# A two-block model on one core: the first block's GpSimd arithmetic moved to VectorE and TensorE

## The chip, the core and the metric

The kernel runs on 1 core of a Trainium2 chip. The metric is the device time of one execution in microseconds (us); the kernel before takes 1670.41 us, the median of three runs (1668.84 to 1670.69). The engines are named as in the profile: PE is TensorE, DVE is VectorE, ACT is ScalarE, POOL is GpSimd, SP is SyncE, which issues most of the loads.

## What is computed

256 tokens of width 1024 pass through two blocks. The first block, the one that matters here, is:

```
mod = silu(c) @ w_ada + b_ada                      # 6 x 1024: sh1, sc1, gt1, sh2, sc2, gt2
h = rms_norm(x, g_norm_mix) * (1 + sc1) + sh1
proj = h @ w_in                                    # q, k, v of 8 forgetting and of 8 stick-breaking heads, 8 gates
log_fcum = cumsum(log_sigmoid(f_logit + b_forget))
forgetting head:      p = softmax(q k / 8 + log_fcum[q] - log_fcum[k], causal);  o = p v
stick-breaking head:  z = q k / 8;  mask k < q
                      rest = reverse cumsum of log_sigmoid(-z) masked to 0, less itself
                      a = exp(log_sigmoid(z) + rest) masked to 0;  o = a v
x = x + gt1 * (norm(o) @ w_out)
h2 = rms_norm(x, g_norm_ffn) * (1 + sc2) + sh2
x = x + gt2 * peer(h2)     # per token and head: scores of 2 x 128 keys, top 16 of 16 x 16,
                           # the 16 chosen rows of expert_down and expert_up (16384 x 1024 each)
```

The second block (a differential and block-sparse attention layer, a gated linear attention layer and two feed-forward layers) follows and is not touched.

## The kernel before

All queues are written out by hand. Each engine has a list of steps (`Queue`), executed strictly in the order in which Python appends them; a step waits on semaphores for its inputs, and everything behind it on that engine waits too. Nothing is scheduled by a planner, so the order of the code is the order on the engines.

**Weights** come as tiles of 1024 x 512 (2 MB) into four buffers W0 to W3. `load_on` issues the loads on SP strictly in the order of the list of tiles, each when the tile that held its buffer is done (`wdone`). The tiles of the first block in order: w_ada 0, 2, 1, 3, w_in 0, 1, 2, w_ada 4, w_in 3, w_ada 5, 6, w_in 4, w_ada 7, w_in 5, w_ada 8, 9, w_out 0, w_query 0, w_out 1, w_query 1, 2, 3, w_ada 10, 11. Products use fp32r operands in two parts: ACT copies a quarter of a tile to WH, and DVE or POOL forms WL = W - WH (`split_piece`, four pieces a tile); a product is then three matmuls for each of 8 row blocks.

**Work beside the products** stands in the deque `behind`: pieces of splits (`later_split`) and, for w_ada tiles 4 to 9, pieces of `ada_rows` (`later_ada`, `later_close`). `tick(n)` puts the next n of them on the engines after a group of matmuls, `take` the rest that a product needs, and `drain` all. `ada_rows` makes one 512-wide piece of the modulation as a row: DVE accumulates the w_ada rows of 4 blocks times silu(c) in LNV, ACT scales the other 4 blocks, POOL adds them up (`sums`), and a product with a matrix of ones (`close`) sums over the partitions; only then is the tile's buffer free.

**Order around the change.** After w_in 0 and 1 (queries and keys of the stick-breaking heads) come w_in 2 (their values), 3 and 4 (forgetting queries and keys); between their groups of 24 matmuls stand the steps of the 8 stick-breaking heads: `sb_first` (scores, ACT abs, exp and ln, two DVE operations, two POOL multiplications by the mask), `sb_second` (the reverse cumulative sum as products, one DVE addition, ACT exp, two POOL multiplications), `sb_third` (the product with the values). Then comes w_in 5 (forgetting values) with the first four of the ten steps of `attention` (scores, reductions, exponents, three transposes of the head before, product with the values) between its halves, and a loop over the rest with `tick(2)` after each. nG holds minus the cumulative log gates for the queries; a DVE operation adds it and the mask to the scores. After the loop come the norms of the heads, the product with w_out, the second norm, and the PEER layer: the query of tokens 0 to 127 with w_query 0, `choose(0, 0, 1)` (the top 16 of the first head, all on DVE), the other query tiles (`first_query`, `query_groups`), then 256 gathers on POOL (1 MB each, 8 buffers of EB) with a DVE dot product (line 78), ACT steps and two products for each. The first gather waits for `tk1`, the end of the second `first_query`; gathers 2 and 3 for w_query 0, 4 and 5 for w_query 2, 6 and 7 for the end of w_query 3, later ones for the product that frees their buffer.

Of the kernel before, what the change touches and what calls it, by code (L numbers as in the profile page):

```python
# [182 lines left out]
def build(nc, A, out, C1, C2):  # L183
    ctx = ExitStack()
    with ctx:
# [32 lines left out]
        with ExitStack() as under:  # L218
            W.append(under.enter_context(nc.sbuf_tensor("W3", [128, 8, 512], F32)))
            WH = [under.enter_context(nc.sbuf_tensor(f"WH{i}", [128, 8, 512], F32R)) for i in range(3)]  # L220
            AH = under.enter_context(nc.sbuf_tensor("AH", [128, 2, 8, 256], F32R))
            AL = under.enter_context(nc.sbuf_tensor("AL", [128, 2, 8, 256], F32R))
        EB = sb("EB", [128, 16384])
# [488 lines left out]
        def ada_rows(j, direct=()):  # L712
# [7 lines left out]
            def some(ks, kp):  # L720
                def step():
# [7 lines left out]
                    for k in kp:  # L729
                        t["a"] = act(lambda e: e.activation(tile.w[:, k, :], tile.w[:, k, :], ACT.Copy, scale=silu_c[:, k:k + 1]),  # L730
                                     t_cb, tile.arrived, ordered=False)
                return step

            def sums():
                w = tile.w
                pool(lambda e: e.tensor_tensor(w[:, 4, :], w[:, 4, :], w[:, 5, :], ALU.add), t["a"])
                if not direct:
                    pool(lambda e: e.tensor_tensor(w[:, 6, :], w[:, 6, :], w[:, 7, :], ALU.add))
                    pool(lambda e: e.tensor_tensor(w[:, 4, :], w[:, 4, :], w[:, 6, :], ALU.add))
                t["p"] = pool(lambda e: e.tensor_tensor(w[:, 4, :], w[:, 4, :], acc, ALU.add), t["d"])  # L740
                acc_free[half] = (t["p"],)
# [13 lines left out]
            a, b = some((0, 1), (4, 5)), some((2, 3), () if direct else (6, 7))  # L755
            return [(cond, a), (cond, lambda: (b(), sums()))], (cond, close)
# [7 lines left out]
        def forget_gates():  # L764
# [21 lines left out]
            yield  # L786
            b = bank()
            mm(PS[b][:, 0:8], [(tri, nl[:, 0, :])], t_nl, *bank_free[b])
            tk = mm(PS[b][:, 8:16], [(ones, nl[:, 0, :]), (tri, nl[:, 1, :])])
            t = dve(lambda e: e.tensor_scalar(nG, PS[b][:, 0:16].rearrange("p (t h) -> p t h", t=2), -1.0, None, ALU.mult), tk)  # L790
            bank_free[b] = (t,)
            t_gates["nG"] = t
            yield
# [43 lines left out]

        gate = forget_gates()
# [11 lines left out]
        def attention(heads, q_of, k_of, v_of, vw, out_bank, scale, LB, PT, maps=1, gates=False, lam=None, tokens=(), base=0, done=None,  # L850
                      taken=None, values_in=lambda: ()):

            NL, NP = len(LB), len(PT)
            MX, SM = (a[:, base:] for a in (MXA, SMA))
            lb_free = [taken() if taken else () for _ in range(NL)]
            pt_free = [taken() if taken else () for _ in range(NP)]
            n = heads
            state = {}
            done["next"] = 0

            def scores(h):
                for m in range(maps):
                    i = h * maps + m
                    b = bank()
                    pe.wait(*tokens, *bank_free[b])
                    for t in range(2):
                        nk = 128 * (t + 1)
                        o = PS[b][:, 128 * t:128 * t + nk]
                        q, k = q_of(i)[:, 128 * t:128 * (t + 1)], k_of(i)[:, 0:nk]
                        if gates:  # L870
                            pe.plain(lambda e, o=o, q=q, k=k: e.matmul(o, q, k, start=True, stop=False))
                            g0 = nl[:, 0, i:i + 1].broadcast_to([128, 128])
                            g1 = nl[:, 1, i:i + 1].broadcast_to([128, 128])
                            if t == 0:
                                tk = pe(lambda e, o=o, g0=g0: e.matmul(o, g0, tri, start=False, stop=True), ordered=False)
                            else:
                                pe.plain(lambda e, o=o, g0=g0: e.matmul(o, g0, tri_ones, start=False, stop=False))
                                tk = pe(lambda e, o=o, g1=g1: e.matmul(o[:, 128:256], g1, tri, start=False, stop=True), ordered=False)
                        else:
                            tk = mm(o, [(q, k)])  # L880
                    L = LB[i % NL]
                    free = lb_free[i % NL]
                    if gates:
                        for t in range(2):
                            c = slice(0, 128) if t == 0 else slice(128, 384)
# [3 lines left out]
                    else:  # L889
                        td = dve(lambda e, b=b, L=L: e.scalar_tensor_tensor(  # L890
                            out=L, in0=PS[b][:, 0:384], scalar=scale, in1=maskF, op0=ALU.mult, op1=ALU.add), tk, *free)
                    bank_free[b] = (td,)
                    for t in range(2):
                        c = slice(0, 128) if t == 0 else slice(128, 384)
                        j = 2 * i + t
                        tm = dve(lambda e, c=c, L=L, j=j: e.tensor_reduce(MX[:, j:j + 1], L[:, c], X_AXIS, ALU.max, negate=True))
                    for t in range(2):
                        c = slice(0, 128) if t == 0 else slice(128, 384)
                        j = 2 * i + t
                        ta = act(lambda e, c=c, L=L, j=j: e.activation(L[:, c], L[:, c], ACT.Exp, bias=MX[:, j:j + 1],  # L900
                                                                       accum_out=SM[:, j:j + 1]), tm, ordered=False)
                    state[i] = ta

            def weights(h):

                tk = [state[h * maps + m] for m in range(maps)]
                j = 2 * h * maps
                tr_ = dve(lambda e: e.reciprocal(SM[:, j:j + 2 * maps], SM[:, j:j + 2 * maps]), *tk)
                if maps == 1:
                    return tk[0]  # L910
# [1314 lines left out]
```

How the kernel before makes its waits and increments, by code:

```python
    def wait(self, *tokens):  # L100
        for sem, value in tokens:
            if value > self.seen.get(sem.name, 0):
                self.seen[sem.name] = value
                self.steps.append(lambda e, s=sem, v=value: e.wait_ge(s, v))
# [1 line left out]
    def __call__(self, make, *tokens, ordered=True):  # L106
        self.wait(*tokens)
        if ordered:
            self.wait(self.last)
        self.n += 1
        self.steps.append(lambda e, m=make(LATER), s=self.sem: m(e).then_inc(s, 1))
        return self.last
# [4 lines left out]
    def dma(self, make, slot, *tokens):  # L118
        self.wait(*tokens)
        slot.n += 16
        self.steps.append(lambda e, m=make(LATER), s=slot.sem: m(e).then_inc(s, 16))
        return (slot.sem, slot.n)
```

## Time and profile before

| | us |
|---|---|
| median of three runs | 1670.41 |
| lowest and highest | 1668.84, 1670.69 |
| the profiled execution | 1669.52 |
| its span on the core | 1667.7 |
| PE busy, share of the span | 1367.8 (82%) |
| DVE busy | 1112.0 (67%) |
| ACT busy | 545.0 (33%) |
| POOL busy | 461.7 (28%) |

The span falls into three stretches: up to about 316 us the first block as far as the last query tile, from there to about 975 us the stream of gathers, and then the second block. Engine shares are averages over these and say little by themselves; each stretch has to be read by what its engines wait for.

### The profile page before, as it was taken

The numbers are of one execution on the slowest core, as the hardware profiler recorded it, in microseconds if no ns is written. First come the engines' busy times: TensorE is split into PE (matmuls) and PEld (weight loads), VectorE is DVE, ScalarE is ACT, GpSimd is POOL, SyncE is SP. The second block draws the span as 40 slices with busy tenths as digits, with TensorE's granted clock in tenths as the row PEclk, the third lists the DMA queues.
The fourth block names the chain that finished last, engine by engine and source line by source line (L and its number), as shares of the span: only waits on it lengthen the run. The fifth ranks groups of instructions, "written<-read, shape, count | busy, mean of one in ns | idle before, by whom it ended". The sixth has DMA issues, their size and how long they took to land.

```text
span 1667.7 us, 17183 instructions
## 1 busy us (share of the span) xinstructions
PE 1367.8 (82%) x6192; PEld 956.3 (57%) x6192; DVE 1112.0 (67%) x2013; ACT 545.0 (33%) x1046; POOL 461.7 (28%) x397
## 2 busy tenths in 40 slices
PE   5887779778777777777777778968999989889997
PEld 5876668523223222322222237856999878679996
DVE  6665756588888678877555555556765577768554
ACT  1454423322221123122111133542544253435431
POOL 1153405245444344444344401100111023001110
PEclk8898889999999899999999988989999999999999
DMA  9554524799999999999999934324555442345450
GB/s 365 194 201 152 202 76 168 288 421 409 421 421 414 417 422 388 384 421 421 421 421 421 422 160 152 102 76 147 184 202 181 174 154 104 124 177 192 173 191 26
DMA packets 116628, 433.16 MB, mean 260 GB/s; under 512 B 6832, under 2 KB 7088, under 8 KB 83520
## 3 DMA queue, kind: packets, MB, share of 16 engines
q0 software_dynamic: 36864, 268.45, 39.0%
q1 hardware_dynamic: 79392, 162.51, 27.4%
q8 instruction: 49, 0.80, 0.2%
q10 hardware_dynamic: 288, 1.11, 0.2%
q14 instruction: 35, 0.29, 0.0%
HBM read 431.00 MB, written 1.05 MB: 259 GB/s over the span
## 4 chain that ended last, share of the span: by engine, by line
PE 48%; DMA 23%; DVE 19%; ACT 6%; issue 2%; POOL 1%; SPq 0%; DVEq 0%; ACTq 0%; POOLq 0%
PE PS L45 47%; DMA EB<-in_experts,EI 22%; DVE EB L78 5%; DVE WL L75 4%; ACT BIG L24 2%; ACT WH L24 1%; PE PS L84 1%; DMA W<-in_w_ada 1%; DVE Y L75 1%; DVE GV L75 1%; DVE XL L75 1%; ACT EB L24 1%; DVE X L63 1%; DVE LNV L63 1%; ACT XH L24 1%
## 5 line engine op out<-in xcount | busy, mean ns | idle before, releaser
L45 PE MATMUL PS<-EB,BIG 128*128 128x512 f32 x1024 | 496.9, 630 | 168.0 <-ACT BIG L24 168.0
L45 PEld LDWEIGHTS PS<-EB,BIG 128*128 128x128 f32 x1024 | 190.8, 197 | 469.4 <-ACT BIG L24 285.0
L78 DVE CUSTOM_DVE_ANT_0 EB<-EB,Y 128x1024 f32<-128x1024 f32 x256 | 313.5, 1224 | 145.8 <-DMA EB<-in_experts,EI 144.6
L39 POOL DMA_INDIRECT EB<-in_experts,EI x256 | 291.2, 1137 | 394.2 <-PE PS L45 378.5
L75 DVE TENSOR_TENSOR WL<-W,WH 128x1024 fp32r<-128x1024 f32 x228 | 297.2, 1352 | 111.4 <-ACT WH L24 111.0
L24 ACT ACTIVATE WH<-W 128x1024 fp32r<-128x1024 f32 x240 | 237.2, 1048 | 81.6 <-PE PS L45 75.8
L45 PE MATMUL PS<-XH,WH 128*128 128x256 f32 x832 | 243.0, 292 | 10.6 <-DVE WL L75 10.0
L45 PE MATMUL PS<-XH,WL 128*128 128x256 f32 x832 | 236.9, 285 | 0.0
L45 PE MATMUL PS<-XL,WH 128*128 128x256 f32 x832 | 236.7, 285 | 0.0
L24 ACT ACTIVATE BIG<-BIG 128x2 f32<-128x2 f32 (+1 forms) x136 | 31.1, 228 | 442.2 <-DVE BIG L78 441.8
L45 PEld LDWEIGHTS PS<-XH,WH 128*128 128x128 f32 x832 | 161.1, 194 | 14.0 <-DVE WL L75 11.1
L45 PEld LDWEIGHTS PS<-XL,WH 128*128 128x128 f32 x832 | 161.2, 194 | 1.9 <-issue 1.4
L45 PEld LDWEIGHTS PS<-XH,WL 128*128 128x128 f32 x832 | 161.2, 194 | 0.0
L45 PE MATMUL PS<-WH,XH 128*128 128x512 f32 x288 | 124.0, 431 | 22.2 <-DVE XL L75 15.2
L75 POOL TENSOR_TENSOR AL<-Y,AH 128x512 fp32r<-128x512 f32 x28 | 36.3, 1296 | 331.2 <-DVE AH L66 331.2
L24 ACT ACTIVATE BIG<-K,BIG 128x128 f32<-128x128 f32 x256 | 100.3, 393 | 59.1 <-DVE BIG L75 57.8
L45 PE MATMUL PS<-WL,XH 128*128 128x512 f32 x288 | 118.4, 411 | 0.0
L45 PE MATMUL PS<-WH,XL 128*128 128x512 f32 x288 | 118.1, 410 | 0.0
L45 PE MATMUL PS<-WL,AH 128*128 128x512 f32 x256 | 101.4, 396 | 0.0
L45 PE MATMUL PS<-WH,AH 128*128 128x512 f32 x256 | 100.8, 394 | 0.0
L45 PE MATMUL PS<-WH,AL 128*128 128x512 f32 x256 | 100.1, 391 | 0.0
L45 PEld LDWEIGHTS PS<-WH,XH 128*128 128x128 f32 x288 | 57.5, 200 | 38.3 <-DVE XL L75 17.7
(176 smaller groups left out, 1496.7 us busy)
## 6 DMA issues: line engine op xcount, KB each, us to landing
W<-in_ffn_w SPq DMA_DIRECT2D x32, 2048.0 KB, 8.5
W<-in_w_ada SPq DMA_DIRECT2D x12, 2048.0 KB, 12.3
W<-in_w_in SPq DMA_DIRECT2D x6, 2048.0 KB, 13.6
W<-in_hy_w_in SPq DMA_DIRECT2D x6, 2048.0 KB, 13.7
W<-in_gla_w_in SPq DMA_DIRECT2D x6, 2048.0 KB, 7.9
W<-in_w_query SPq DMA_DIRECT2D x4, 2048.0 KB, 10.4
W<-in_w_out SPq DMA_DIRECT2D x2, 2048.0 KB, 8.0
EB<-in_experts,EI POOLq DMA_INDIRECT x256, 11.2
```

The costliest lines, as they stand in the source:

```text
L24: return lambda e: e.activation(*a, **k)
L39: return lambda e: e.indirect_dma_start(*a, **k)
L45: return lambda e: e.matmul(*a, **k)
L63: return lambda e: e.scalar_tensor_tensor(*a, **k)
L75: return lambda e: e.tensor_tensor(*a, **k)
L78: return lambda e: e.tensor_tensor_reduce(*a, **k)
L84: return lambda e: e.transpose(*a, **k)
```

## The change

- `ada_rows`: DVE accumulates 6 blocks instead of 4 (three pieces of two blocks in `behind`, before two pieces), the last two blocks are products of silu(c), broadcast, with the tile (fp32, 512 columns each), and `close` adds the product of ones with LNV. ACT's scaling and POOL's sums are gone.
- Stick-breaking heads: the four POOL multiplications are gone; a product of the identity with a strict mask (0 or -1e30), both fp32r in the new tile MR, is added to the scores of each of the two diagonal tiles.
- Forgetting heads: the function `attention` becomes `forgetting`. The causal mask is a product of the identity with 384 columns, the row maxima are read from PSUM, and ACT takes the exponent from PSUM. The two DVE operations that added nG and the mask are gone, and so is the calculation of nG.
- The WL parts of w_out 1, w_query 1 and w_query 2 are made by DVE instead of POOL.
- `choose(0, 0, 1)` stands ahead of `drain()` instead of behind it.

```diff
@@ ada_rows
-            def some(ks, kp):
+            def some(ks):
...
-                    for k in kp:
-                        t["a"] = act(lambda e: e.activation(tile.w[:, k, :], tile.w[:, k, :], ACT.Copy, scale=silu_c[:, k:k + 1]),
-                                     t_cb, tile.arrived, ordered=False)
...
-            def sums():
-                w = tile.w
-                pool(lambda e: e.tensor_tensor(w[:, 4, :], w[:, 4, :], w[:, 5, :], ALU.add), t["a"])
...
-                t["p"] = pool(lambda e: e.tensor_tensor(w[:, 4, :], w[:, 4, :], acc, ALU.add), t["d"])
...
             def close():
                 b = bank()
-                tk = mm(PS[b][:, :], [(silu_c[:, k:k + 1].broadcast_to([128, 128]), tile.w[:, k, :]) for k in direct] +
-                        [(ones, tile.w[:, 4, :])], t["p"], *bank_free[b])
+                tk = mm(PS[b][:, :], [(silu_c[:, k:k + 1].broadcast_to([128, 128]), tile.w[:, k, :]) for k in (6, 7)] + [(ones, acc)],
+                        t["d"], tile.arrived, *bank_free[b])
...
-            a, b = some((0, 1), (4, 5)), some((2, 3), () if direct else (6, 7))
-            return [(cond, a), (cond, lambda: (b(), sums()))], (cond, close)
+            return [(cond, some((0, 1))), (cond, some((2, 3))), (cond, some((4, 5)))], (cond, close)
@@ forgetting, scores
-                            td = dve(lambda e, c=c, t=t, b=b, L=L, i=i: e.scalar_tensor_tensor(
-                                out=L[:, c], in0=PS[b][:, c], scalar=nG[:, t, i:i + 1], in1=maskF[:, c],
-                                op0=ALU.add, op1=ALU.add), tk, *free)
...
+                pe.plain(lambda e: e.matmul(PS[b][:, 0:384], ident_a, causal_a, start=True, stop=False))
...
+                    tm = dve(lambda e: e.tensor_reduce(MXA[:, 2 * h + t:2 * h + t + 1], PS[b][:, cols[t]], X_AXIS, ALU.max, negate=True),
+                             tk, ordered=False)
@@ sb_first
-            pool(lambda e: e.tensor_tensor(zb[:, 0:128], zb[:, 0:128], maskS, ALU.mult), dd)
-            zst[h] = (pool(lambda e: e.tensor_tensor(zb[:, 256:384], zb[:, 256:384], maskS, ALU.mult)), dd)
+            pe.plain(lambda e: e.matmul(PS[b][:, 0:128], ident_a, strict_a, start=False, stop=True))
...
+            zst[h] = (dd,)
@@
-        later_split(wout[1], pool)
+        later_split(wout[1])
...
-        later_split(wq[1], pool)
-        later_split(wq[2], pool)
+        later_split(wq[1])
+        later_split(wq[2])
         next(query)
         tick(1)
         norm_x1.last()
         t_xt = norm_x1.tokens
         next(query)
-        drain()
         for step in choose(0, 0, 1):
             step()
+        drain()
```

What it moves on DVE is told here at three places. The names are those of the buffers: W, WH and WL with the buffer's number, LNV the accumulator of `ada_rows`, PS the PSUM banks, ST the row maxima, EB the exponents.

DVE between the first two forgetting heads, before: w_in 5 has just begun, and w_ada 8 (in W0) and w_ada 9 (in W3) are accumulated behind the maxima of head 0.

```order
L75 TENSOR_TENSOR GV<-GV,PS0 128x512
L63 SCALAR_TENSOR_TENSOR EB<-PS2,ST,K1 128x128
L63 SCALAR_TENSOR_TENSOR EB<-PS2,ST,K1 128x256
L69 TENSOR_REDUCE ST<-EB 128x1 x2
L66 COPY BIG<-PS1 128x512
L72 TENSOR_SCALAR LNV<-W0,ST 128x512
L63 SCALAR_TENSOR_TENSOR LNV<-W0,ST,LNV 128x512 x3
L72 TENSOR_SCALAR LNV<-W3,ST 128x512
L63 SCALAR_TENSOR_TENSOR LNV<-W3,ST,LNV 128x512 x3
```

The same place in the changed kernel, up to the maxima of head 1 and 2.

```order
L69 TENSOR_REDUCE ST<-PS0 128x1 x2
L66 COPY BIG<-PS3 128x512
L75 TENSOR_TENSOR GV<-GV,PS1 128x512
L72 TENSOR_SCALAR LNV<-W0,ST 128x512
L63 SCALAR_TENSOR_TENSOR LNV<-W0,ST,LNV 128x512 x5
L72 TENSOR_SCALAR LNV<-W3,ST 128x512
L63 SCALAR_TENSOR_TENSOR LNV<-W3,ST,LNV 128x512
L69 TENSOR_REDUCE ST<-PS2 128x1 x2
L60 RECIPROCAL ST<-ST 128x2
L66 COPY EB<-PS3 128x384
L69 TENSOR_REDUCE ST<-PS1 128x1 x2
```

The addition of the closed w_ada 7 row (GV) used to stand ahead of head 0's maxima and now stands behind them, and the maxima of head 1 stand behind the first two of the six operations on w_ada 9.

DVE in the loop over the forgetting heads, in the changed kernel: the splits of w_out 0 (WL0) and w_out 1 (WL3) between the maxima of heads 5, 6 and 7.

```order
L75 TENSOR_TENSOR WL0<-W0,WH0 128x1024 x2
L69 TENSOR_REDUCE ST<-PS1 128x1 x2
L60 RECIPROCAL ST<-ST 128x2
L66 COPY EB<-PS2 128x384
L75 TENSOR_TENSOR WL0<-W0,WH0 128x1024
L75 TENSOR_TENSOR WL3<-W3,WH1 128x1024
L69 TENSOR_REDUCE ST<-PS3 128x1 x2
L60 RECIPROCAL ST<-ST 128x2
L69 TENSOR_REDUCE ST<-PS6 128x8
L75 TENSOR_TENSOR WL3<-W3,WH1 128x1024 x2
```

Before, all four WL0 pieces stood together ahead of head 3, and there was no WL3 piece on DVE at all. Now one WL0 piece stands ahead of head 3's maxima and seven pieces follow in the loop.

DVE around `choose(0, 0, 1)`, the difference: from MAX to the CAST into EI it is the choice of the first head, WL1 is of w_query 1 and WL0 of w_query 2.

```order
 L63 SCALAR_TENSOR_TENSOR Y<-Y,ST,GV 128x512 x2
+L75 TENSOR_TENSOR WL<-W,WH 128x1024
 L75 TENSOR_TENSOR XL<-PS,XH 128x4x128 x2
 L48 MAX LNV<-BIG 128x8
```

```order
 L63 SCALAR_TENSOR_TENSOR LNV<-LNV 128x16
 L66 CAST EI<-LNV 128x16
+L75 TENSOR_TENSOR WL<-W,WH 128x1024 x7
 L78 ISA EB,BIG<-EB,Y 128x1024
```

One WL piece now stands ahead of the last XL parts, and the other seven stand behind the whole choice; before, POOL made all eight.

## Rows read from the trace of the kernel before

**Rows 1.** Windows: us, busy time (instructions) of each engine, granted clock, DMA share, GB/s.

```profile
300.00:316.00 16.00, 15.02 (x94) 12.88 (x94) 12.53 (x36) 2.57 (x6) 0.00 (x0) 0.91 0.37 142
400.00:500.00 100.00, 74.76 (x161) 28.78 (x162) 83.65 (x211) 24.05 (x69) 47.33 (x41) 1.00 1.01 421
```

**Rows 2.** Timeline of POOL: start, us, operation, idle time before and its releaser.

```profile
257.81 19.18 POOL L75 TENSOR_TENSOR WL<-W,WH 128x1024 fp32r<-128x1024 f32 x8 [50.33 <-ACT WH L24]
281.31 1.11 POOL L39 DMA_INDIRECT EB<-in_experts,EI  x1 [4.33 <-PE PS L45]
316.61 0.94 POOL L39 DMA_INDIRECT EB<-in_experts,EI  x1 [22.00 <-PE PS L45]
```

**Rows 3.** Timeline of PE, rows that begin after a wait or mark a stage.

```profile
71.73 0.83 PE L45 MATMUL PS<-ST,K 128*128 128x8 f32 x6 [1.68 <-DVE ST L75]
126.67 0.58 PE L45 MATMUL PS<-XH,WH 128*128 128x256 f32 x1 [3.44 <-DVE WL L75]
170.31 1.22 PE L45 MATMUL PS<-W,K 128*128 128x512 f32 x1 [8.84 <-POOL W L75]
191.81 0.90 PE L84 MATMUL PS<-K,EB 128*128 128x128 f32 x3 [5.33 <-ACT EB L24]
209.77 0.63 PE L84 MATMUL PS<-K,Y 128*128 128x128 f32 x2
259.59 0.50 PE L45 MATMUL PS<-WH,XH 128*128 128x512 f32 x1 [1.60 <-DVE XL L75]
268.23 0.60 PE L84 MATMUL PS<-K,EB 128*128 128x128 f32 x4
307.00 1.98 PE L45 MATMUL PS<-EB,BIG 128*128 128x512 f32 x4 [0.98 <-ACT BIG L24]
```

**Rows 4.** Groups by form, 60 to 280 us: busy, mean ns, idle before.

```profile
L24 ACT ACTIVATE WH<-W 128x1024 fp32r<-128x1024 f32 x36 | 35.8, 1050 | 1.6 <-DMA W<-in_w_in 1.4 <-issue 0.2
L75 DVE TENSOR_TENSOR WL<-W,WH 128x1024 fp32r<-128x1024 f32 x24 | 29.5, 1266 | 15.3 <-ACT WH L24 15.3
L45 PE MATMUL PS<-BIG 128*128 128x128 f32 x32 | 7.2, 311 | 0.0
```

**Rows 5.** Timeline of DVE in the heads and splits of the first block.

```profile
94.00 2.55 DVE L63 SCALAR_TENSOR_TENSOR LNV<-W,ST,LNV 128x512 f32<-128x512 f32 x3
184.37 4.62 DVE L75 TENSOR_TENSOR WL<-W,WH 128x1024 fp32r<-128x1024 f32 x4
189.09 0.87 DVE L63 SCALAR_TENSOR_TENSOR EB<-PS,ST,K 128x128 f32<-128x128 f32 x2
190.00 0.74 DVE L69 TENSOR_REDUCE ST<-EB 128x1 f32<-128x128 f32 x2
```

**Rows 6.** Timeline of DVE in the choice of experts: beside POOL's splits, and later without.

```profile
265.09 2.56 DVE L75 TENSOR_TENSOR GV<-LNV 128x256 f32<-128x256 f32 x1
270.20 4.45 DVE L72 TENSOR_SCALAR LNV<-LNV 128x16 uint32<-128x16 uint32 x2
280.22 0.17 DVE L66 CAST EI<-LNV 128x16 int32<-128x16 f32 x1
311.84 0.42 DVE L75 TENSOR_TENSOR GV<-LNV 128x256 f32<-128x256 f32 x1
330.05 0.39 DVE L72 TENSOR_SCALAR LNV<-LNV 128x16 uint32<-128x16 uint32 x2
```

**Rows 7.** DMA issues by SP in a short window: KB each, us to landing.

```profile
W<-in_w_out SPq DMA_DIRECT2D x1, 2048.0 KB, 7.9
```

**Rows 8.** Windows, columns as in rows 1: four stretches of the first block.

```profile
75.33:153.69 78.36, 65.54 (x374) 58.12 (x373) 44.88 (x57) 37.57 (x61) 34.01 (x45) 0.87 0.45 161
153.69:209.77 56.08, 39.53 (x212) 33.62 (x210) 39.11 (x71) 25.29 (x59) 21.43 (x12) 0.86 0.52 188
191.80:198.00 6.20, 6.19 (x29) 5.90 (x30) 2.27 (x7) 3.88 (x8) 1.72 (x1) 0.57 0.70 254
268.23:292.16 23.93, 23.24 (x198) 22.83 (x196) 13.05 (x22) 4.19 (x7) 12.68 (x8) 1.00 0.74 284
```

More of the change, by code:

```diff
@@ L222, in build @@
             AL = under.enter_context(nc.sbuf_tensor("AL", [128, 2, 8, 256], F32R))
+        with ExitStack() as under:
+            under.enter_context(nc.sbuf_tensor("EB_a", [128, 15744], F32))
+            MR = under.enter_context(nc.sbuf_tensor("MR", [128, 640], F32R))
         EB = sb("EB", [128, 16384])
@@ L848, in build, with forgetting @@
         t_sb_in = (act.last, dve.last, pool.last)
[L850 to L857, printed above, removed]
+        def forgetting(LB, PT, values_in, *tokens):
+            lb_free = [(fox_done["sb"],) for _ in LB]
+            pt_free = [(fox_done["sb"],) for _ in PT]
@@ L858, in attention @@
             state = {}
-            done["next"] = 0
+            cols = [slice(0, 128), slice(128, 384)]
             def scores(h):
[L862 to L885, printed above, removed]
-                            td = dve(lambda e, c=c, t=t, b=b, L=L, i=i: e.scalar_tensor_tensor(
-                                out=L[:, c], in0=PS[b][:, c], scalar=nG[:, t, i:i + 1], in1=maskF[:, c],
-                                op0=ALU.add, op1=ALU.add), tk, *free)
[L889 to L910, printed above, removed]
[L911 to L918 removed]
+                b = bank()
@@ new lines, in scores @@
+                pe.wait(*tokens, t_ident, *bank_free[b])
+                pe.plain(lambda e: e.matmul(PS[b][:, 0:384], ident_a, causal_a, start=True, stop=False))
+                g0, g1 = (nl[:, t, h:h + 1].broadcast_to([128, 128]) for t in range(2))
+                k = KF[:, h // 2, :]
+                pe.plain(lambda e: e.matmul(PS[b][:, 0:128], QF[:, h, 0:128], k[:, 0:128], start=False, stop=False))
+                pe.plain(lambda e: e.matmul(PS[b][:, 0:128], g0, tri, start=False, stop=False))
@@ L920, in turned @@
+                L = LB[h % len(LB)]
+                for t in range(2):
+                    j = 2 * h + t
+                    ta = act(lambda e: e.activation(L[:, cols[t]], PS[b][:, cols[t]], ACT.Exp, bias=MXA[:, j:j + 1], accum_out=SMA[:, j:j + 1]),
+                             tm, *lb_free[h % len(LB)], ordered=False)
+                bank_free[b] = (ta,)
+                state[h] = ta
             def turned(h):
-                tk = weights(h)
-                L = LB[(h * maps) % NL]
+                dve(lambda e: e.reciprocal(SMA[:, 2 * h:2 * h + 2], SMA[:, 2 * h:2 * h + 2]), state[h])
@@ L946, in attention @@
+                v = lambda t: V[:, t, h * 64:(h + 1) * 64]
+                mm(PS[4][:, h * 64:(h + 1) * 64], [(P[:, 0:128], v(0))], state["pt", h], *values_in(), *bank_free[4], *bank_free[5])
+                tk = mm(PS[5][:, h * 64:(h + 1) * 64], [(P[:, 128:256], v(0)), (P[:, 256:384], v(1))])
+                pt_free[h % len(PT)] = (tk,)
+                return tk
+            after_values = 0
+            for i in range(10):
+                if i < 8:
                     scores(i)
-                if 0 <= i - 1 < n:
+                if 0 <= i - 1 < 8:
@@ L1027, in build @@
         fm_tile(win[4], evac_copy(lambda c: KF[:, c:c + 2, :]), hook=step_sb)
-        fox = attention(8, lambda i: QF[:, i, :], lambda i: KF[:, i // 2, :],
-                        lambda h, t: V[:, t, h * 64:(h + 1) * 64], 64, 4, 1.0,
-                        [buf(i) for i in (6, 7, 8, 9)], [buf(i) for i in (0, 1, 2, 3, 4)],
-                        gates=True, tokens=(act.last, dve.last, t_gates["nG"]), done=fox_done, taken=lambda: (fox_done["sb"],),
-                        values_in=lambda: t_vf)
+        fox = forgetting([buf(i) for i in (5, 6, 7, 8)], [buf(i) for i in (0, 1, 2, 3, 4)], lambda: t_vf, act.last, dve.last, t_gates["nl"])
         later_ada(8)
```

70 lines of the change are left out of this document (27 added, 43 removed).

## The prediction, made before the changed kernel ran

> **What bounds the kernel now.** I read the windows first, then the timelines of POOL, PE and DVE up to 330 us. In the middle stretch the DMA engines are full: 421 GB/s at a share of 1.01 from 400 to 500 us, with DVE busy for 84 of 100 us [rows 1]. The stream begins for good at 316.61 us, when POOL has waited 22 us for PE [rows 2]: it waits for the end of w_query 3, which frees the last two gather buffers. Just before it, from 300 to 316 us, the DMA share is 0.37 [rows 1]. So the first block is worth to the total exactly what it does to the end of w_query 3, and nothing behind that point changes: same gathers, same order, same second block. DVE's or POOL's busy time in the first block is worth nothing by itself. Up to that point the path is PE's queue with its waits: 3.44 us for a WL part at 126.67, 8.84 us for POOL's sums at 170.31, 5.33 us for ACT's exponents at 191.81 [rows 3]. From 75.33 to 153.69 PE is busy for 65.54 of 78.36 us at a mean clock of 0.87, that is for about 20 us at the lower of its two levels, 1.2 instead of 2.4 GHz [rows 8].
>
> **Part 1, to the end of w_ada 7's product.** Before, this is at 153.69 us, where the window of 78.36 us ends. Of the 78.36 us in front of it 12.8 are waits; the low clock takes half of some 20 us, 10.2; PE's work at full clock is 65.5 - 10.2 = 55.3 us [rows 8]. Nearly all of the waits come from POOL or ACT's scaling, and they go. The products for nG (0.83 us, 0.7 without the pipeline) with the wait of 1.68 us ahead of them go too [rows 3]: 2.4 us, so that the stretch begins at 72.9 (estimate from the start of the products at 75.33). Added on PE: an fp32 product of 512 columns is two records, and four take 1.98 us [rows 3], so some 0.86 to 0.99 us each; two more for each of four tiles are 6.9 us. The 16 mask products of 128 columns are in no row. An fp32 product of this width is two records, and the records run one behind another at some 0.11 us, well under the mean of 0.311 us that contains the pipeline [rows 4]; I bound one mask product by 0.06 and 0.21 us and take 0.13, 2.1 us in all (1.0 to 3.4). The order also puts 24 matmuls of w_in 5 (5.6), the scores of the first forgetting head (1.7) and one sb_third (0.6) ahead of this product, which stood behind it: 7.9 us. New waits: w_in 4's first group needs WL parts that stand on DVE behind the close of w_ada 5 and behind a head's DVE and ACT work, as at 126.67 before [rows 3]; walking DVE's and ACT's queues there gives 6.1 us more than the group takes, with 0.8 us each for a bank and for the clock behind it: 7.9 us with rounding. The sum: 72.9 + 55.3 + 6.9 + 2.1 + 7.9 + 7.9 = 153.0 us. **Gain 0.7 us** (2.6 more if the clock stays up).
>
> DVE's 12 added accumulations are 0.85 us each, three in 2.55 us [rows 5]; in this part DVE is busy for 44.9 of 78.4 us [rows 8] and has the room.
>
> **Part 2, from there to the first transposes of the heads' norm (209.77).** Before: 56.08 us [rows 8], of which 8.84 is the wait for POOL's sums [rows 3]. That wait goes, but two loads take its place. w_ada 9 is loaded into the buffer that this product frees, and a lone 2 MB load lands after 7.9 us [rows 7]. Before, DVE had the maxima of head 1 behind all of w_ada 9, too, but PE was held by POOL anyway. Now: 8.0 (landing), 1.6 (two DVE operations), 0.8 (maxima of head 1, 0.74 in [rows 5]), 1.0 (exponents on ACT), 0.3 (hand-overs), then on PE 0.5 (transposes), 2.8 (12 matmuls), 2.6 (closing w_ada 8): 17.6 us. Only then can w_out 0 be loaded: 8.0, then WH 1.05 on ACT, WL 1.2 on DVE [rows 4], and behind it in DVE's queue the maxima of head 3, 0.75, and ACT's exponents, 1.0: 12.0 us to the transposes of head 3, the place of 191.81 before. From there the loop took 18.0 us, to 209.77 [rows 3]. In it stand now seven WL pieces of 1.16 us (four in 4.62) and five times 0.87 us for nG and mask less [rows 5], 8.1 - 4.4 = 3.7 us more of DVE work. Because each pair of pieces waits for its WH copies and holds the next head's maxima, I walked the queues step by step: exponents of head 5 end at 8.0, of head 6 at 14.4, of head 7 at 20.0, the last WL piece at 23.3, the row of norms at 24.8 us. 17.6 + 12.0 + 24.8 = 54.4 us. **Gain 1.7 us**; if the clock falls behind the first of these waits, as it did behind 191.81 (0.57 for 6.2 us [rows 8]), a loss of 1.1.
>
> **Part 3, norms to w_query 0.** The same steps on the same engines, but one WL piece now ahead of the XL parts on which the product at 259.59 waits; ACT's copy for it is ready, so it moves them by what it takes less a gap of 0.5 us: **loss 0.7 us**.
>
> **Part 4, the query tiles.** This is the largest term. Before, the 24 matmuls of w_query 0 and the first 24 of w_query 1 end at 268.23, 8.64 us after 259.59 [rows 3], while POOL makes the WL parts in 2.40 us each [rows 2]. Now three of the four WL pieces of w_query 1 stand on DVE behind `choose(0, 0, 1)`. That took 20.7 us, from 259.6 to the cast at 280.22 [rows 6]. Three groups of its rows were long beside POOL: the addition 2.56 instead of 0.42, the two shifts 4.45 instead of 0.39 us [rows 6], and the casts around them likewise; with the later durations of the same rows it takes 10.8 us. Then WL: 12.0, 13.1, 14.3 us, and 0.7 us for the last matmuls: 15.0 us instead of 8.6, **loss 6.4 us**. PE has no slack to return it: from 268.23 to 292.16 us it is busy for 23.2 of 23.9 us [rows 8], and w_query 3's end follows from there. The clock may fall behind this wait of 5.6 us, which costs 2.4 us more; I take half, 1.2. The choice is ready ten microseconds earlier, but the first gather waits for the second query's scores, which stand on PE behind this wait. It was issued at 281.31 before [rows 2], 21.7 us after 259.59; now, by PE, at some 21.9 us: it hardly moves.
>
> **Sum:** -0.7 - 1.7 + 0.7 + 6.4 + 1.2 = +5.9 us, on the profiled execution's 1669.5: 1675.4. The median of the runs is 0.9 us above it: **1676.3 us**.
>
> **A rule that speaks for the change.** DVE's rows beside POOL were slow: 4.45 against 0.39 us [rows 6]. The Trainium skill, GPSIMD Engine Reference, Specifications, says that GpSimd shares its SBUF interfaces with VectorE and contends with instructions that have two SBUF inputs or run in a two-port mode. On this the trace agrees. The rule with the choice taken as the path would give these ten microseconds as a gain, some 1660 us; by the rows they only shorten the wait of part 4, and its chance is within that of rival A.
>
> **The rivals.** *A: DVE has room and PE keeps its lead.* DVE is busy for 39.1 of 56.1 us in part 2 [rows 8], and its rows get shorter without POOL. If the splits fit into the loop's gaps, it stays at 18.0 us, 6.8 less than I walked, and with the clock up in part 1 2.6 more goes, and the 1.2: 1676.3 - 10.6 = 1665.7, faster. It decides at whether the loop ends within 20 us of head 3's transposes. Against it: the WL pieces stand in queue ahead of maxima, and ACT's copies ahead of exponents. *B: the wait in part 4 is made up* before w_query 3: PE waits 3 us for WL of w_query 3 and about 1 us for ACT behind it, and parts 1 and 2 are at their better ends. About -5 us: 1671, no change. Against it: these waits hang on the scores of w_query 2, which are late as well. *C: the clock falls behind each new wait* (parts 2 and 4) and mask products cost 0.21 us: +2.8, +1.2, +1.3, 1681.6.
>
> **Chances.** The forecast with its near surroundings (1673.8 to 1679) 0.47, C 0.19, B 0.21, A 0.13. A measurement of this kernel can tell some 0.2%, 3.3 us, from no change. Faster by more: 0.13; within: 0.22; slower by more: 0.65. The range is from inside A, 1666, to beyond C, 1683.
>
> **What would show it.** In the changed profile: no ACT or POOL wait on PE up to 150 us, w_ada 7 closed near 153; a wait of some 4 us for ACT before head 1's transposes and of 5 to 6 before head 3's; the norm's first transposes near 208; PE waiting 5 to 6 us for WL in the first group of w_query 1, right behind the products of w_query 0, while DVE runs the choice in about 11 us; the stream of gathers restarting near 322 and as long as before. It would be wrong if that first group ran without a wait, or if the loop of the forgetting heads took less than 20 us.

## The result, and the profile after

The changed kernel takes 1675.7 us (median of 12 runs, 1672.1 to 1678.6), the kernel before 1668.6 us (12 runs, 1666.0 to 1671.6) beside it. The ratio is 1.0040, 95% interval 1.0028 to 1.0051: **slower by 4.7 to 8.5 us**. The forecast was +5.9 us and 1676.3 us. Most times below come from one profiled execution of each kernel. The profiled execution of the changed kernel took 1672.6 us.

The stages of the prediction, as windows of the changed kernel: to the close of w_ada 7, from there to the norm's first transposes, the loop over the forgetting heads inside that, the first product with w_query 0, the way from its second product to the end of w_query 1's first group, the last 18 of the 24 matmuls of that group, and the way on to the stream. The columns are those of [rows 1].

```profile
72.60:152.14 79.54, 73.79 (x446) 62.73 (x445) 48.55 (x68) 31.43 (x53) 0.00 (x0) 0.98 0.45 159
152.14:207.29 55.15, 38.24 (x187) 31.93 (x185) 31.88 (x59) 18.47 (x46) 0.00 (x0) 0.81 0.53 191
182.66:207.29 24.63, 18.18 (x97) 16.84 (x97) 15.38 (x29) 13.69 (x31) 0.00 (x0) 0.71 0.49 180
246.97:254.38 7.41, 7.41 (x24) 5.56 (x24) 5.06 (x11) 1.13 (x4) 0.00 (x0) 0.77 0.01 2
259.81:275.76 15.95, 10.44 (x49) 9.16 (x50) 14.94 (x43) 6.17 (x7) 0.00 (x0) 0.79 0.39 131
271.87:275.76 3.89, 3.89 (x19) 3.89 (x20) 3.89 (x4) 0.00 (x0) 0.00 (x0) 0.52 0.25 91
275.76:323.87 48.11, 42.26 (x318) 39.05 (x316) 20.32 (x46) 13.09 (x22) 5.80 (x7) 0.96 0.58 219
```

POOL does nothing in these windows up to the gathers. The timeline of PE shows the waits that have come in place of those for POOL in [rows 3], with the rows that mark the stages.

```profile
72.60 0.40 PE L45 MATMUL PS<-WH,XH 128*128 128x512 f32 x1
...
118.09 0.39 PE L45 MATMUL PS<-XH,WH 128*128 128x256 f32 x1 [3.98 <-DVE WL L75]
...
149.41 1.88 PE L45 MATMUL PS<-W,ST 128*128 128x512 f32 x4
151.12 1.02 PE L45 MATMUL PS<-LNV,K 128*128 128x512 f32 x2
...
163.45 0.90 PE L84 MATMUL PS<-K,EB 128*128 128x128 f32 x3 [4.80 <-ACT EB L24]
...
182.66 0.90 PE L84 MATMUL PS<-K,EB 128*128 128x128 f32 x3 [5.66 <-ACT EB L24]
...
207.29 1.12 PE L84 MATMUL PS<-K,Y 128*128 128x128 f32 x4 [0.89 <-DVE Y L75]
...
259.81 0.50 PE L45 MATMUL PS<-WH,XH 128*128 128x512 f32 x1 [2.24 <-DVE XL L75]
...
271.87 0.58 PE L45 MATMUL PS<-XH,WH 128*128 128x256 f32 x1 [5.51 <-DVE WL L75]
```

PE's two waits for ACT's exponents, at 163.45 and 182.66 us, go back to two loads. DVE waits 3.25 us for the landing of w_ada 9, of which two operations stand ahead of the maxima of head 1. ACT waits 10.08 us for the landing of w_out 0, whose first split piece stands ahead of the maxima of head 3.

```profile
160.65 0.49 DVE L72 TENSOR_SCALAR LNV<-W,ST 128x512 f32<-128x512 f32 x1 [3.25 <-DMA W<-in_w_ada]
161.17 0.75 DVE L63 SCALAR_TENSOR_TENSOR LNV<-W,ST,LNV 128x512 f32<-128x512 f32 x1
161.84 0.61 DVE L69 TENSOR_REDUCE ST<-PS 128x1 f32<-128x128 f32 x2
```

```profile
178.82 1.06 ACT L24 ACTIVATE WH<-W 128x1024 fp32r<-128x1024 f32 x1 [10.08 <-DMA W<-in_w_out]
```

DVE at the choice of the first head: one WL piece, the XL parts, the choice with the two shifts in it, and then the WL pieces for which PE waits.

```profile
257.33 1.23 DVE L75 TENSOR_TENSOR WL<-W,WH 128x1024 fp32r<-128x1024 f32 x1 [4.08 <-ACT WH L24]
258.47 1.28 DVE L75 TENSOR_TENSOR XL<-PS,XH 128x512 fp32r<-128x512 f32 x2
259.86 0.30 DVE L48 MAX8 LNV<-BIG 128x8 f32<-128x128 f32 x1
...
266.73 0.39 DVE L72 TENSOR_SCALAR LNV<-LNV 128x16 uint32<-128x16 uint32 x2
...
270.52 0.17 DVE L66 CAST EI<-LNV 128x16 int32<-128x16 f32 x1
270.60 8.03 DVE L75 TENSOR_TENSOR WL<-W,WH 128x1024 fp32r<-128x1024 f32 x7
```

And POOL, the first gather and the one that begins the stream:

```profile
280.35 1.11 POOL L39 DMA_INDIRECT EB<-in_experts,EI  x1 [217.29 <-PE PS L45]
...
323.87 0.94 POOL L39 DMA_INDIRECT EB<-in_experts,EI  x1 [21.73 <-PE PS L45]
```

The choice takes 10.83 us instead of 20.75 [rows 6], and the first gather leaves 1 us earlier. The stream begins 7.26 us later than at 316.61 [rows 2], and the last gather leaves at 969.45 instead of 961.41. The two profiled spans differ by 3.1 us only: in the one of before the last eight products on the gathered rows ran at the lower clock, for 6.38 instead of 3.70 us, and the four before them took 3.09 instead of 1.98 us, 3.8 us together. The medians differ by 7.2 us.

### The profile page after: what moved, and what is told of

Same layout as the page of the kernel before. It is cut to its first block, busy times and chain, and to the rows that moved or that the text cites. A ratio compares the mean times of both kernels' runs of the same rounds, so it can differ in the third digit from the quotient of the medians.

```text
span 1670.8 us, 17135 instructions
## 1 busy us (share of the span) xinstructions
PE 1381.0 (83%) x6234; PEld 967.0 (58%) x6234; DVE 1106.2 (66%) x2021; ACT 530.4 (32%) x1024; POOL 378.5 (23%) x329
## 4 chain that ended last, share of the span: by engine, by line
PE 48%; DMA 24%; DVE 19%; ACT 5%; issue 2%; SPq 0%; POOL 0%; DVEq 0%; ACTq 0%; POOLq 0%
PE PS L45 47%; DMA EB<-in_experts,EI 22%; DVE EB L78 5%; DVE WL L75 4%; ACT BIG L24 2%; DMA W<-in_w_ada 1%; ACT WH L24 1%; PE PS L84 1%; DVE Y L75 1%; DVE GV L75 1%; DVE LNV L63 1%; DVE XL L75 1%; ACT EB L24 1%; DVE X L63 1%; DVE ST L69 1%
## 5 line engine op out<-in xcount | busy, mean ns | idle before, releaser
L75 DVE TENSOR_TENSOR WL<-W,WH 128x1024 fp32r<-128x1024 f32 x240 | 310.3, 1341 | 119.4 <-ACT WH L24 119.0
L45 PEld LDWEIGHTS PS<-WH,XH 128*128 128x128 f32 x288 | 57.8, 201 | 39.2 <-DVE XL L75 18.4
## 6 DMA issues: line engine op xcount, KB each, us to landing
W<-in_w_ada SPq DMA_DIRECT2D x12, 2048.0 KB, 12.8
EB<-in_experts,EI POOLq DMA_INDIRECT x256, 11.3
```

The source lines that it names most:

```text
L45: return lambda e: e.matmul(*a, **k)
L75: return lambda e: e.tensor_tensor(*a, **k)
```

## The experiments

Two theories stood against each other. The first is the forecast's: what is late is PE's way to the end of w_query 3, through DVE's queue order, so the parts can be undone there. The second: the parts that moved to PE and DVE cost by themselves. Here is where each kernel stood in its profiled execution. "Head 3" is the start of its transposes, "norm" that of the norm's first transposes, the loop is the difference, "stream" is the gather after the long wait for PE; ratios are to the kernel before, with 95% intervals. The places are of one execution each; the column "stream" holds 1.6 us that go with the clock in the first product with w_query 0 and not with the edits (last section): that product was at full clock in the kernel before, in the early close with the splits on POOL, in the rows in two pieces and in both kernels with the rows as before.

| kernel | head 3 | norm | loop | stream | ratio |
|---|---|---|---|---|---|
| before | 191.81 | 209.77 | 18.0 | 316.61 | 1 |
| changed | 182.66 | 207.29 | 24.6 | 323.87 | 1.0040 (1.0028 to 1.0051) |
| WL of w_query 1 first | 183.35 | 207.98 | 24.6 | 317.37 | 1.0004 (0.9995 to 1.0013) |
| all WL pieces first | 183.60 | 207.84 | 24.2 | 318.82 | 0.9999 (0.9988 to 1.0010) |
| w_out 1 on POOL | 184.42 | 207.16 | 22.7 | 324.87 | 1.0047 (1.0035 to 1.0059) |
| all old splits on POOL | 183.04 | 205.77 | 22.7 | 313.94 | 0.9993 (0.9983 to 1.0002) |
| w_ada 8 closed early | 183.82 | 207.23 | 23.4 | 323.08 | 1.0030 (1.0018 to 1.0041) |
| closed early, splits on POOL | 181.74 | 203.24 | 21.5 | 310.15 | 0.9960 (0.9947 to 0.9973) |
| rows in two pieces | 184.44 | 203.36 | 18.9 | 318.17 | 0.9996 (0.9979 to 1.0014) |
| rows as before | 179.53 | 197.96 | 18.4 | 313.61 | 0.9960 (0.9947 to 0.9973) |
| rows as before, WL of w_query 1 first | 178.97 | 197.82 | 18.8 | 305.13 | 0.9925 (0.9904 to 0.9946) |
| masks alone | 179.99 | 197.18 | 17.2 | 306.23 | 0.9911 (0.9891 to 0.9930) |
| rows alone | 188.49 | 213.71 | 25.2 | 322.53 | 1.0023 (1.0009 to 1.0037) |

**The order at the choice.** Two kernels differ from the changed one only here.

```diff
+        take(wq[1])
         for step in choose(0, 0, 1):
             step()
         drain()
```

> The changed kernel with one edit: the four WL pieces of w_query 1 are made ahead of the choice of the first head, those of w_query 2 stay behind it. My theory: PE's wait of 5.51 us in the first group of w_query 1 is DVE's queue order and nothing else. It then goes whole, the 24 matmuls of w_query 0 and the first 24 of w_query 1 take 8.6 to 9.5 us instead of 15.95, the long gather stream restarts at 316.5 to 318 us instead of 323.87, and the time falls by 6 to 7 us, to that of the kernel before (ratio to it 0.999 to 1.001). Rival 1, a landing or ACT's WH copies hold the group: a wait of over 3 us stays, the ratio stays at 1.004. Rival 2, the wait is only moved to a later product (the choice is now later by 3.5 us): the group is short, the restart stays near 323.

The second has `drain()` ahead of the loop, as before.

> The changed kernel with the old order of the two lines: all seven WL pieces (w_query 1 and 2) ahead of the choice, which ends some 8 to 10 us later than 270.69. My theory, that only PE's path to the end of w_query 3 counts: the same as with w_query 1 alone ahead, restart 316.5 to 318 us, ratio 0.999 to 1.001; the first gather may come some us later than 280.35 and this costs nothing. Rival, that the early indices were worth something: the time is 2 to 4 us above that of the kernel with only w_query 1 ahead, because the first gathers are late.

Both as expected in the times; the two groups take 8.50 us, just under the 8.6 forecast, and the second kernel's stream begins at 318.82 us, 0.8 us behind the latest forecast. The window of the two products, with w_query 1's WL pieces first, is 8.50 us at full clock, where the changed kernel has 15.95:

```profile
260.57:269.07 8.50, 8.50 (x49) 7.42 (x49) 8.02 (x24) 6.17 (x7) 0.00 (x0) 1.00 0.15 34
```

The time falls by 0.36 to 0.41% of 1668.6, 6.0 to 6.8 us: part 4 of the prediction is settled. With all pieces first the first gather leaves at 279.66 instead of 275.79 us, and the two times are the same within their intervals: no gain of early indices can be seen here.

**The splits of w_out 1.**

```diff
-        later_split(wout[1])
+        later_split(wout[1], pool)
```

> The changed kernel with the WL parts of w_out 1 on POOL, as before; everything else stays on DVE. My theory: DVE's pieces ahead of the heads' maxima make the loop over the forgetting heads long (24.6 us from head 3's transposes to the norm's first transposes, 18.0 before). Three or four of eight pieces leave DVE: the loop takes 19 to 21 us, and the time falls by 3.5 to 5.5 us (ratio 1.001 to 1.002). Rival, ACT's WH copies ahead of the exponents set the loop, whoever subtracts: it stays at 23.5 to 24.6 us and the time does not move (1.004).

Missed. POOL has the four pieces, and the loop is shorter by 1.9 us, not by 3.6 to 5.6; of the time nothing came back.

```profile
196.07 2.45 POOL L75 TENSOR_TENSOR WL<-W,WH 128x1024 fp32r<-128x1024 f32 x1 [132.01 <-ACT WH L24]
199.18 6.96 POOL L75 TENSOR_TENSOR WL<-W,WH 128x1024 fp32r<-128x1024 f32 x3 [0.67 <-ACT WH L24]
```

DVE's part in w_out 1 is thus a small term; neither theory named the large one. This execution was 1.0 us late at the group of 118.09 already, 1.8 us at head 3, and the stream began 1.0 us later than in the changed kernel; by the two intervals a gain of more than 2 us is as good as excluded.

**All old splits on POOL again.**

```diff
-        later_split(wout[1])
+        later_split(wout[1], pool)
...
-        later_split(wq[1])
-        later_split(wq[2])
+        later_split(wq[1], pool)
+        later_split(wq[2], pool)
```

> The changed kernel with all WL parts that POOL made before (w_out 1, w_query 1 and 2) on POOL again; the modulation rows and both masks stay as changed. My theory: the loop shortens as with w_out 1 alone, the wait of 5.5 us in the first group of w_query 1 goes, and DVE's choice is slow again beside POOL (20 us instead of 10.8) without cost, since the first gather waits for PE. Restart at 312 to 314 us, the time 3 to 6 us below the kernel before (ratio 0.9965 to 0.998). Rival, the rows on PE and the masks cost by themselves: the ratio is 1.000 or above.

The wait in part 4 is gone, and the choice is slow again:

```profile
267.79 4.47 DVE L72 TENSOR_SCALAR LNV<-LNV 128x16 uint32<-128x16 uint32 x2
...
277.81 0.17 DVE L66 CAST EI<-LNV 128x16 int32<-128x16 f32 x1
```

4.47 us for the pair of shifts against 0.39 without POOL: the choice takes 20.7 us beside POOL in this kernel and 10.8 in the changed one. The addition in it with both inputs in the SBUF took 2.57 us at 262.67 against 0.42. That agrees with the Trainium skill, GPSIMD Engine Reference, Specifications, by which GpSimd and VectorE share their SBUF interfaces and contend when a VectorE instruction has two SBUF inputs or runs in a two-port mode. The shifts have one tensor input, and in which mode they run no trace shows. The slow choice costs the kernel nothing, as PE does not wait for it. The ratio, 0.9993, lies outside the 0.9965 to 0.998 that was expected, although the stream begins at 313.94 us, within the forecast 312 to 314: masks and rows together gain next to nothing even with the splits undone. So something in them costs, and that was the open question for the rest.

**The early close of w_ada 8.**

```diff
         later_ada(8)
-        later_ada(9)
         later_close(8)
+        later_ada(9)
```

> The changed kernel with the close of w_ada 8 ahead of the accumulation of w_ada 9 in the deque. Theory: in part 2 two landings of 2 MB stand on the path, one after the other (w_ada 9 ahead of the maxima of head 1, w_out 0 ahead of those of head 3), because w_ada 8 is closed only at 170.7 us. Closed ahead of w_ada 9 (DVE has its sums at 157.4, so PE waits some 5 us for them at 152), w_out 0 is issued near 160 and lands near 168, and no maxima wait for a landing: head 3's transposes near 178 to 179 instead of 182.66, the waits of 4.80 and 5.66 us for ACT's exponents gone. The time falls by 4 to 6 us (ratio to before 1.0005 to 1.002, from 1.004). Rival: the waits there are queue work of DVE and ACT, not landings; then the new wait of 5 us at 152 comes on top and the time is the same or 3 to 5 us longer.

The landings are indeed off the path, and PE waits for DVE's sums instead, with the products behind that wait at the lower clock (3.78 us where they took 1.88):

```profile
159.02 3.78 PE L45 MATMUL PS<-W,ST 128*128 128x512 f32 x4 [5.31 <-DVE LNV L63]
```

The two waits of 4.80 and 5.66 us for ACT's exponents are gone (0.38 us is left at 183.82), so they were landings, as the theory had it. Waits of 5.31 and 2.40 us for DVE's sums and the lower clock take their place: head 3 comes at 183.82, no earlier than before the edit, and the intervals of the two times overlap. The rival had the outcome right and the reason wrong. With the splits on POOL the same edit was tried again:

> Both edits together: the close of w_ada 8 ahead of w_ada 9 and the WL parts of w_out 1, w_query 1 and 2 on POOL again. If the two add, the restart of the stream comes 4 to 6 us earlier than with the splits on POOL alone (there 3 us ahead of the kernel before), so 7 to 9 us ahead of the kernel before, and the ratio is 0.995 to 0.997. Rival, the order gives nothing once the loop has room: 0.999 as with the splits on POOL alone.

The ratio, 0.9960, is as expected, and 0.3% below that with the splits on POOL alone. The stream begins 3.8 us earlier, just short of 4 to 6; 1.6 us of this are the first product with w_query 0, at full clock here, and 2.5 us show at the norm.

**The price of a mask product.** Each of the 16 is issued four times.

> The changed kernel with each mask product of the stick-breaking heads made four times instead of once (48 more products of 128 columns; the masked scores are -4e30 instead of -1e30, which changes nothing in what follows). Measures one mask product: the forecast took 0.13 us (bounds 0.06 and 0.21), the trace of the changed kernel suggests 0.10 us. The stretch from the first product of V to the close of w_ada 7 (79.5 us) then grows by 4.8 us at 0.10, by 6.2 at 0.13, by 10 at 0.21, if PE's waits there stay the same.

```profile
72.36 0.40 PE L45 MATMUL PS<-WH,XH 128*128 128x512 f32 x1
...
155.38 1.02 PE L45 MATMUL PS<-LNV,K 128*128 128x512 f32 x2
```

The stretch from 72.36 to the end of this row, 156.40, is 84.04 us instead of 79.54: 4.50 us for 48 products, 0.094 us each. The wait for WL is the same, 3.99 us, but PE's other waits in the stretch are 0.5 us less; its busy time grows from 73.79 to 78.75 us, which is 0.10 us each. This is from one profile; the kernel's time, 1682.5 us, is a single run.

**The modulation rows as before.** `ada_rows` is that of the kernel before, with ACT's scaling and POOL's sums; all else is as changed.

> The changed kernel with the modulation rows made as before (four blocks on DVE, four on ACT, three sums and one more on POOL, one product of ones); masks, forgetting heads, splits and the order of the choice as changed. Theory: products in place of POOL's sums gain in part 2 what the landings then take back, so undoing them brings back the wait of some 9 us for POOL before the close of w_ada 8 and some waits in part 1, and saves 6.9 us of PE in part 1 and 3.4 us in part 2; the time changes by -2 to +3 us against the changed kernel (ratio 1.003 to 1.006). Rival, the eight more fp32 products of 512 columns are what makes the changed kernel slow: then this one is 5 us or more faster than it (ratio 1.001 or below).

The time is the rival's, and by more than it said: 0.8% faster than the changed kernel, 0.4% faster than before, although the wait for POOL's sums is back (7.89 us at 158.28) and part 4 still waits 5.51 us. Its cause, the products, is not shown by this kernel alone: the edit takes away the third piece of each tile too (below). With w_query 1's WL pieces first as well:

> The modulation rows as before and w_query 1's WL pieces ahead of the choice; masks, forgetting heads and DVE's splits as changed. Without the second edit the stream restarted at 313.61 us, the first group of w_query 1 still waited 5.51 us, and the ratio was 0.996. Theory: the two edits add, since both lie on PE's way to the end of w_query 3: restart at 307 to 308.5 us, ratio 0.992 to 0.993 (near 1657 us). Rival: something else, a load for one, bounds the start of the stream by now, and the ratio stays at 0.995 to 0.996.

The two edits add: the ratio, 0.9925, is as expected, and the stream begins at 305.13 us, earlier than the 307 to 308.5 forecast.

**One part alone.** Masks and forgetting heads as changed; rows, splits and the order at the choice as before:

> One part of the change alone: both kinds of masks as products and the new forgetting heads; modulation rows, POOL's splits and the order of the two lines as before. Theory: this part carries the whole gain: restart 306 to 309 us (before 316.61), ratio 0.991 to 0.994. Rival: masks and heads give little, and the gain of the kernel with old rows came from the splits on DVE: ratio 0.997 to 1.000.

As expected. This part carries the whole gain, and it is the fastest of these kernels: 1656.6 us, 0.9911. PE still waits for POOL's sums,

```profile
158.73 2.08 PE L45 MATMUL PS<-W,K 128*128 128x512 f32 x2 [7.89 <-POOL W L75]
```

but all PE waits from 70 to 200 us fall from 28.6 us before to 21.6 us, and the loop is at its shortest:

```profile
179.99:197.18 17.19, 15.95 (x97) 14.98 (x97) 7.26 (x22) 10.75 (x28) 9.32 (x4) 0.80 0.32 117
```

The opposite: the kernel before with the new rows alone.

> The kernel before with the new modulation rows alone (three pieces of two blocks on DVE, two blocks as products, no ACT scaling, no POOL sums). Theory: this part alone is the loss: 6.9 us of products in part 1 and 3.8 in part 2, waits for POOL's sums gone but landings in their place, and the third piece of each tile pushes w_out 0's splits into the loop over the forgetting heads: ratio 1.004 to 1.008. Rival: without the masks on PE the waits for POOL that go are worth more than the products, ratio 0.999 to 1.002.

Slower by 1.5 to 6.2 us, less than expected: the interval ends at 1.0037, the forecast began at 1.004. Both waits that the forecast had for the changed kernel are there, and are longer:

```profile
167.09 0.90 PE L84 MATMUL PS<-K,EB 128*128 128x128 f32 x3 [6.11 <-ACT EB L24]
...
188.49 0.90 PE L84 MATMUL PS<-K,EB 128*128 128x128 f32 x3 [7.16 <-ACT EB L24]
```

The parts don't add. Alone the masks are worth -14.9 us and the rows +3.8 (ratios times 1668.6), together, with the splits on POOL, -1.2: rows on top of masks cost 13.7 us. One reason can be read from the sums of PE's waits from 70 to 200 us: 28.6 us before, 21.6 with the masks alone, 21.5 with the rows alone, 18.3 with both and the splits on POOL. Each part alone takes 7 us of waits away, both together 10.3. So the rows on top save 3.3 us, and they bring twelve fp32 products of 512 columns, two for each of six tiles, at 1.88 us a pair: 11.3 us. That gives +8.0, an estimate, as the kernels are up to 12 us apart within this window. More is in the loop, next.

**The third piece.** The six accumulations of a w_ada tile in two pieces of `behind`, as many as before:

```diff
-            return [(cond, some((0, 1))), (cond, some((2, 3))), (cond, some((4, 5)))], (cond, close)
+            return [(cond, some((0, 1, 2))), (cond, some((3, 4, 5)))], (cond, close)
```

> The changed kernel with the six accumulations of a w_ada tile in two pieces of three instead of three pieces of two; all products, masks and splits as changed. Then the same places in the deque are left for the splits as before: all four WL pieces of w_out 0 stand ahead of head 3 and four of w_out 1, not seven pieces, in the loop. Theory: the loop falls from 24.6 to 18 to 20 us, and the time by 4 to 7 us (ratio 1.000 to 1.0015). Rival: the products for the rows themselves make the changed kernel slow: the loop's length moves but head 3 comes later by the same, ratio 1.003 to 1.005.

As expected, or a little more: 0.44% faster than the changed kernel by the ratios, and the loop at 18.9 us. The WL pieces of DVE around the loop, in the changed kernel,

```profile
179.91 1.23 DVE L75 TENSOR_TENSOR WL<-W,WH 128x1024 fp32r<-128x1024 f32 x1 [5.20 <-ACT WH L24]
...
185.87 2.36 DVE L75 TENSOR_TENSOR WL<-W,WH 128x1024 fp32r<-128x1024 f32 x2 [2.03 <-ACT WH L24]
...
193.31 2.36 DVE L75 TENSOR_TENSOR WL<-W,WH 128x1024 fp32r<-128x1024 f32 x2 [2.56 <-ACT WH L24]
...
198.50 2.36 DVE L75 TENSOR_TENSOR WL<-W,WH 128x1024 fp32r<-128x1024 f32 x2 [1.38 <-ACT WH L24]
...
204.46 1.23 DVE L75 TENSOR_TENSOR WL<-W,WH 128x1024 fp32r<-128x1024 f32 x1 [1.48 <-ACT WH L24]
```

and with two pieces:

```profile
178.28 4.62 DVE L75 TENSOR_TENSOR WL<-W,WH 128x1024 fp32r<-128x1024 f32 x4
...
187.65 2.36 DVE L75 TENSOR_TENSOR WL<-W,WH 128x1024 fp32r<-128x1024 f32 x2 [2.04 <-ACT WH L24]
...
195.09 2.36 DVE L75 TENSOR_TENSOR WL<-W,WH 128x1024 fp32r<-128x1024 f32 x2 [2.56 <-ACT WH L24]
```

Each pair of pieces in the loop first waits 1.4 to 2.6 us for two WH copies on ACT and then holds the next head's maxima. A third piece for each w_ada tile uses up places of `tick`, so three of w_out 0's splits more stand in the loop. With two pieces all four run in one go of 4.62 us ahead of head 3's transposes, which come 1.8 us later for it, and the loop is 5.7 us shorter: 3.9 us at the norm. The closes move as well. w_ada 7 is closed at 146.66 us instead of 152.14, so w_ada 9 has landed when DVE comes to it, and PE waits 5.32 us for DVE's sums and 3.79 us for head 3's exponents where it waited 4.80 and 5.66 us.

This kernel and the one with the rows as before both have two pieces for a tile and the same splits, so between them stands the arithmetic of the rows alone: the norm at 203.36 against 197.96 us, the stream at 318.17 against 313.61, the ratio 0.9996 against 0.9960. Of the 9.3 us at the norm that the new rows cost the changed kernel, 3.9 are the third piece and 5.4 the products in place of POOL's sums.

## Why the prediction was right, and where it was not

**The sum** was +5.9 us; at the start of the stream it is +7.26, in the medians +6.7 by the ratio. By its own terms, with the measured one behind each: part 1 -0.7, -1.6; part 2 -1.7, -0.9; part 3 +0.7, +2.7; part 4 with the clock +7.6, +7.3; behind it 0, -0.3 (48.11 us instead of 48.38 from the group's end to the stream). They add up to +7.2, within rounding. The path, the places of the waits and the largest term were right. That the forecast median, 1676.3, is only 0.6 us off is luck in part: the kernel before took 1668.6 us beside the changed one and not the 1670.4 from which the forecast started, and the misses of the terms, +2.0, +0.8, -0.9, -0.3 and -0.3 us, cancel in part.

**Part 1.** The forecast had the close of w_ada 7 end at 153.0 us; it ends at 152.14. The start at 72.9 was 72.60. The mask product, taken at 0.13 us, is 0.10, 0.5 us less for the sixteen. The fp32 products are 0.94 us each, as bounded. Of the ACT and POOL waits that were to go, two of 0.49 and 0.31 us for ACT are left up to 150 us, and the one of 3.98 us for WL is that of the walk, which made it 6.1. The granted clock is 0.98 for the stretch, 0.87 before [rows 8]. All waits are 5.8 us (79.54 less 73.79), the clock costs some 1.6 us (an estimate from 0.98), together 7.3 where the forecast had 7.9. One reading was wrong: "nearly all" of the 12.8 us of waits before were said to be POOL's or ACT's scaling. Those were 7.6 us; 5.1 us were for DVE, and 5.0 us for DVE are still there.

**Part 2.** Both landings came as walked: head 1's transposes after 4.80 us (some 4 forecast), head 3's at 182.66 (17.6 + 12.0 us behind the close, so 181.7), the loop at 24.6 (24.8). 55.15 us in all, 54.4 forecast. The clock did fall in the loop, 0.71 where before it was 0.79, but PE waits there anyway. The walk was right, and so was its reason, pieces that wait for their copies and hold the next maxima. What the text did not ask is why seven pieces stand in the loop. DVE's added work is the small part: w_out 1 on POOL gives back 1.9 us of the loop. Two pieces for each w_ada tile give back 5.7 us with not one DVE operation less. It is the place of the pieces, set by the third piece of each tile.

**Part 3** was mis-sized: 0.7 us forecast, 2.7 measured from the norm's transposes to 259.81. The one WL piece ahead of XL is what it was said to be, PE waits 2.24 us instead of 1.60. The first product with w_query 0 took 7.41 us at a clock of 0.77, where before it was:

```profile
248.97:254.81 5.84, 5.83 (x24) 4.42 (x24) 4.62 (x11) 1.13 (x4) 0.00 (x0) 1.00 0.00 1
```

That is 1.6 us; the forecast had the clock as a risk in parts 2 and 4 only. The other 1.1 us are 0.5 up to that product and 0.6 for the longer wait.

**Part 4** was the largest term and the best one: 15.95 us from the start of the second product to the end of the group (15.0 forecast and 1.2 for half a fall of the clock). PE waits 5.51 us while DVE runs the choice in 10.83 (10.8 forecast), and the clock behind the wait is 0.52 for 3.89 us, where the same 18 matmuls take about half at full clock. The clock fell in full and still cost only about 0.9 us, by an estimate: the last WL piece is ready some 14.3 us after 259.81, so at full clock the group would have ended at 15.0 to 15.1 all the same. That half of 2.4 us fits is thus luck. Two kernels undo the whole term for 6.0 to 6.8 us.

**The rivals.** A needed a loop under 20 us; it took 24.6. B had the wait made up before w_query 3: from the group's end to the stream 0.3 us came back. C priced mask products at 0.21 us; they are 0.10. Its clock half came true as an event, behind the waits of parts 2 and 4, but not at its price, and a fall in part 3 that no rival had named cost more. What the text nowhere weighed is that a part of the change costs on top of the other: masks alone would have given the kernel 0.9%.

**Left open.** Masks alone gain 14.9 us by the ratio, 10.4 at the stream's start and 9.9 between the two profiled executions. Of this the waits on PE are 7.0 us; the rest would be the clock (0.95 from 72.60 to 141.56, 0.87 before in [rows 8]) and the products for nG, which no run took apart; nor do the runs tell the masks of the stick-breaking heads from the new forgetting heads. The 13.7 us that rows cost on top of masks are 7.7 at the stream's start (3.1 up to head 3, 5.5 in the loop, 0.9 back behind it) and 9.8 between the profiled executions. The sizes found for it, 11.3 us of products, 3.3 us of waits less, 5.7 us for the third piece, add up to 13.7, but they overlap (the waits reach into the loop), so this is no account of it, and between 7.7 and 13.7 the size stays open.

## What to carry to other kernels

Before work goes from an idle engine to a busy one, ask whether anyone still waits for it once the other parts of the change are in: two parts that remove the same waits don't add up in what they gain, but each brings its whole cost. In a queue filled by counts, one more piece of a job moves everything behind it; look at what is pushed into the stage where the other engines wait for each other. And an operation put ahead of a split that a product needs can cost that product's engine most of its duration (here 7.3 of 10.8 us), while an earlier result that nobody waits for gives nothing.

## What the hardware showed that was not expected

The same 24 matmuls with w_query 0, behind the same wait of 2.0 us for XL, took 7.4 us in eight of the fourteen profiled executions and 5.8 to 5.9 us in the other six. The changed kernel is among the eight, the one with fourfold masks, which is the same from 80 us before that point on, among the six. What decides it was not found. As each kernel has one profile, no run shows whether it changes between executions of one kernel; it is 1.6 us that the edits don't explain, and it was most of the miss in part 3.

Behind a wait of 4.6 to 8.8 us PE ran at the lower clock each time that one is found in the fourteen profiles between 60 us and the stream: the three transposes took 0.90 instead of 0.49 us at 163.45 and 182.66, the rows' products 3.78 instead of 1.88 us at 159.02 in the kernel with the early close. In part 4 a wait of 5.51 us came with a stretch 7.3 us longer.
